# A gated recurrence: the diagonal and the first level as one product of 256 columns, in two halves of the heads

## The chip, the cores and the metric

The kernel runs on one core of a Trainium2 chip. The metric is the device time of one execution in microseconds (us), lower is better.

## What is computed

The reference is four blocks of a small language model over 256 tokens of width 1024, one after another: stick-breaking attention with a convolutional feed-forward block, forgetting attention with another feed-forward block, windowed attention, and last a gated recurrence. Only this last block is touched by the change. Cut to what matters:

```
q = silu(h @ Wq);  log_f = log(lb + (1-lb)*sigmoid(h @ Wf));  k = 1 - exp(log_f);  v = h @ Wi
S_t = exp(log_f_t) * S_(t-1) + k_t v_t^T          # per head, 8 heads, keys 128, values 128
o_t = q_t . S_t
o   = o * rsqrt(mean(o*o) + eps) * gnorm * silu(h @ Wz)
out = o @ W_out                                   # then rmsnorm and residual
```

Without the state it is a product over pairs: o_t is the sum over s <= t of (q_t . (k_s times the product of the forget factors from s+1 to t)) v_s. That is how the kernel computes it.

## The kernel before, in words

**Weights.** All weight matrices come as one stream of units of 128x2048 numbers. SyncE loads a unit, ScalarE rounds it to its high part (line 491), VectorE subtracts to get the low part (line 970, in `split_lo`, called in order by `split_to`), and TensorE multiplies three times (lines 1739 to 1741). Three units have room at a time, so a high part can be made only when the unit three before it is used up. Each engine works through a list of instructions in the order in which it is written, and semaphores tie the lists together.

**The recurrence in levels.** The 256 tokens of the 8 heads make 16 tiles of 128 tokens ("key tiles": `kk_tiles[i]`, with the query tiles beside them). Inside a tile the pairs (s, t) fall into the diagonal (s = t) and seven levels of block size m = 1, 2, 4, ..., 64: in level n a late block of m tokens looks at the early block beside it. For each level TensorE multiplies all 16 key tiles with the late half of the query tiles (`level`, line 2451, 64 columns each). VectorE then copies the entries that belong to this level into the score tiles (`pick`, line 1632, a copy under a mask) and multiplies queries and keys by the forget factors of their neighbouring block (`decay`, lines 1599 and 1600), with which the next level works. The factors of whole blocks, `totals`, are made by pairwise products (`block_totals`, line 1607, one instruction of 1024 elements and five shorter ones, each waiting for the one before). The diagonal has a product of its own, `level_diagonal` (line 2439): the bare queries `qT` against the same key tiles, 128 columns each, picked by `pick_diagonal` (line 1618). Level 1 uses the queries times their own forget factor, `X[0]`, made by `first_queries` (line 1590). These products are in plain float32, for which the program issues each matmul as two passes (16 matmuls are 32 instructions in the trace).

**Order on TensorE.** The products of the recurrence are put between those of the value and gate projections (`rec_i`, `rec_z`). These are 16 parts of 12 matmuls of 512 columns each (`token_rows`). The table `AFTER` says what follows which part: the diagonal after part 1, level 1 after part 2, level n after part n + 1, the product across the two tiles of a head (`cross`) after part 9, the outputs (`outputs(0)`, `outputs(1)`, lines 2472 and 2475) after part 10, the transposes of the first half of the gated outputs (`turn_outputs(0)`, line 2486) after part 15. After part 16 comes the output projection, `last_rows`, which waits for `olo`, the low part of the transposed outputs (line 1711).

**Order on VectorE around the change** (by line in the trace): the first queries of heads 0 to 3 (1590), the scaling of the second half of the queries out of PSUM (1124, two instructions), a split (970), the first queries of heads 4 to 7 (1590), a split (970), `pick_diagonal` (1618, two instructions), `block_totals` (1607), `decay(1)`, `pick(1)`, a split, and so on. After the outputs: sums and means of squares (1686, 1689), whose power -1/2 GpSimd takes (469), a split (`split_to(ro)`), the outputs scaled out of PSUM (`out_scaled`, line 1696, four instructions), the scaling of the gate's first half (1109), `gain_gate` (1678), which waits for a Silu on ScalarE, `out_gated` (1705), two splits, `out_lo` (1711).

**PSUM.** `psD` has four banks of 512 columns. Levels alternate between banks 0, 1 and banks 2, 3, and level n waits until the pick of level n - 2 has read its banks (`rec["picked"]`).

Of the kernel before, what the change touches and what calls it, by code (L numbers as in the profile page):

```python
# [27 lines left out]
ACT = mybir.ActivationFunctionType  # L28
AX = mybir.AxisListType

P = 128
D = 1024
T = 256
TT = T // P
# [7 lines left out]
REC_H = 8  # L42
# [46 lines left out]
def build(nc, stream, pvec, post_g, x_in, wf, bf, b_in, b_out, sinks, gnorm, pos, out):  # L89
    with ExitStack() as ctx:  # L90
# [3 lines left out]
        def sem(name):  # L94
            return ctx.enter_context(nc.semaphore(name))
# [10 lines left out]
        qT = sb("qT", [P, KT, T])  # L106
# [4 lines left out]
        arena = sb("arena", [P, 11264])  # L111
# [93 lines left out]
              for s in ("fox", "win")]  # L205
# [1 line left out]
        rope = {n: sem(f"rope_{n}") for n in ("arg", "sin", "applied", "turned", "copied")}  # L207
        gate = {n: sem(f"gate_{n}") for n in ("z", "tanh", "made")}
        ffn = [{n: sem(f"ffn{i}_{n}") for n in ("scaled", "centre", "tap1", "gate", "up", "gelu", "g", "g_hi", "g_lo")} for i in range(2)]
        rec = {n: sem(f"rec_{n}") for n in ("bound", "bounds", "sigmoid", "silu", "cleared", "ready", "decayed", "total", "level", "cross", "crossed",  # L210
                                            "picked", "gate", "o", "osq", "sums", "omean", "oscale", "scaled", "gated", "turned", "ohi", "olo")}
        stored = sem("stored")

# [261 lines left out]
        def _(act):  # L475
# [415 lines left out]
            def query_silu(c):  # L891

                act.wait_ge(chunk_freed_v, V_FREED[E0["rec_q"] + c])
                part = qT[:, 4 * c:4 * c + 4, :]
                nc.scalar.activation(part, part, ACT.Silu).then_inc(rec["silu"], 1)

            def gate_silu(c):

# [51 lines left out]
        def _(dve):  # L950
# [8 lines left out]
            V = nc.vector  # L959
# [157 lines left out]
            def evac_features(name, c, dst, scale=None, signal=None, first=0):  # L1117

                chunk_wait(name, c)
                for b in range(2):  # L1120
                    k = 4 * (c - first) + 2 * b
                    src, out_ = along(bank(E0[name] + c, b)), dst[:, k:k + 2, :]
                    if scale is None:
                        ins = V.tensor_tensor(out_, src, row_bc, ALU.mult)
                    else:
                        ins = V.scalar_tensor_tensor(out_, src, scale, row_bc, ALU.mult, ALU.mult)
                    if signal is not None and b == 0:
                        ins.then_inc(signal, 1)
                ins.then_inc(chunk_freed_v, 1)
                if signal is not None:  # L1130
                    dve.wait_ge(chunk_freed_v, V_FREED[E0[name] + c])
                    V.memset(st[:, 0, 3, :], 0.0).then_inc(signal, 1)
# [446 lines left out]
                    ins = V.tensor_scalar(head(kk, k), head(kk, k), lbv[:, 2, k:k + 1], None, ALU.mult)  # L1579
                ins.then_inc(rec["ready"], 1)  # L1580

            q_all = qT[:, :, :].rearrange("p k t -> p (k t)")
            QA = X[0]

            def first_queries(c):

                half = slice(1024 * c, 1024 * c + 1024)
                dve.wait_ge(rec["silu"], c + 1)
                dve.wait_ge(rec["ready"], c + 1)
                V.tensor_tensor(QA[:, half], q_all[:, half], keep_f[:, half], ALU.mult).then_inc(rec["decayed"], 1)  # L1590
# [12 lines left out]
            def block_totals():  # L1603

                for n in range(1, 7):
                    total = totals[n - 1].rearrange("p (b two) -> p b two", two=2)
                    V.tensor_tensor(totals[n], total[:, :, 0], total[:, :, 1], ALU.mult).then_inc(rec["total"], 1)
                    dve.wait_ge(rec["total"], n)

            tiles = sc_diag.rearrange("p (g t) -> p g t", t=P)  # L1610

            def pick_diagonal():

                dve.wait_ge(consts_pool, N_CONSTS)
                dve.wait_ge(rec["level"], 1)
                dve.wait_ge(rec["cleared"], 1)
                for half in range(2):
                    ins = V.copy_predicated(tiles[:, 8 * half:8 * half + 8, :], mask_level[:, 0, :].unsqueeze(1).to_broadcast([P, 8, P]),
                                            psD_rows[:, half, :].rearrange("p (g t) -> p g t", t=P))
                ins.then_inc(rec["picked"], 1)  # L1620

            def pick(n):

                m = LEVELS[n - 1]
                nb = P // (2 * m)
                dve.wait_ge(rec["level"], n + 1)
                dve.wait_ge(rec["picked"], n)
                out_ = tiles.rearrange("p g (b two m) -> p g b two m", two=2, m=m)[:, :, :, 1, :]
                mask = mask_level[:, n, :].rearrange("p (b two m) -> p b two m", two=2, m=m)[:, :, 1, :]
                at = 2 * (n % 2)  # L1630
                got = psD[:, at:at + 2, :].rearrange("p k n -> p (k n)").rearrange("p (g b m) -> p g b m", b=nb, m=m)
                V.copy_predicated(out_, mask.unsqueeze(1).to_broadcast([P, TT * REC_H, nb, m]), got).then_inc(rec["picked"], 1)
# [10 lines left out]
            evac_features("rec_q", 0, qT)  # L1643
            split_to(ri + 1)
            first_queries(0)
            evac_features("rec_q", 1, qT)
            split_to(ri + 2)
            first_queries(1)
            split_to(ri + 3)
            pick_diagonal()  # L1650
            block_totals()
            decay(1)
            pick(1)
            split_to(ri + 4)
            decay(2)
            pick(2)
# [56 lines left out]

            out_mean(0)
            out_mean(1)
            split_to(ro)
            out_scaled(0)
            out_scaled(1)
            evac("rec_z", 0, hn[:, 0, 0:512], 5)
            gain_gate(0)  # L1720
            out_gated(0)
# [12 lines left out]
        def _(pe):  # L1734
# [696 lines left out]

            kk_tiles, query_tiles = ([a[:, P * i:P * i + P] for i in range(TT * REC_H)] for a in (kk, X[0]))

            def level_diagonal():

                pe.wait_ge(rec["ready"], 2)
                pe.wait_ge(rec["silu"], 2)
                for i in range(TT * REC_H):
                    ins = MM(psD[:, i // 4, P * (i % 4):P * (i % 4) + P], kk_tiles[i], qT[:, i // 2, P * (i % 2):P * (i % 2) + P],
                             start=(i % 4 == 0), stop=True, skip_group_check=True)  # L2440
                ins.then_inc(rec["level"], 1)

            def level(n):

                m = LEVELS[n - 1]
                pe.wait_ge(rec["decayed"], n + 1)
                pe.wait_ge(rec["picked"], max(n - 1, 1))
                for i in range(TT * REC_H):
                    late = query_tiles[i].rearrange("p (b two m) -> p b two m", two=2, m=m)[:, :, 1, :]
                    at = 64 * (i % 8)  # L2450
                    ins = MM(psD[:, 2 * (n % 2) + i // 8, at:at + 64].rearrange("p (b m) -> p b m", m=m), kk_tiles[i], late,  # L2451
                             start=(i % 8 == 0), stop=True, skip_group_check=True)
                ins.then_inc(rec["level"], 1)
# [25 lines left out]
            def turn_outputs(b):  # L2479
# [3 lines left out]
                for tt in range(TT):  # L2483
                    pe.wait_ge(rec["gated"], 2 * b + tt + 1)
                    for k in range(4):
# [1 line left out]
                                                  X[1][:, tt * D + 512 * b + k * P:tt * D + 512 * b + k * P + P], ident[:, :])  # L2487
                    ins.then_inc(rec["turned"], 1)

            AFTER = {1: [level_diagonal], 2: [lambda: level(1)], 3: [lambda: level(2)], 4: [lambda: level(3)], 5: [lambda: level(4)],  # L2490
                     6: [lambda: level(5)], 7: [lambda: level(6)], 8: [lambda: level(7)], 9: [cross],
                     10: [lambda: outputs(0), lambda: outputs(1)], 15: [lambda: turn_outputs(0)]}
            part = 0
            for name, c in (("rec_i", 0), ("rec_i", 1), ("rec_z", 0), ("rec_z", 1)):
                e = E0[name] + c
# [119 lines left out]
```

## Time and profile before

| | |
|---|---|
| time, median of 3 runs | 911.25 us (911.05 to 911.58) |
| the profiled execution's own time | 911.09 us |
| its span in the trace | 909.4 us |
| TensorE (matmul) busy | 892.2 us, 98% |
| TensorE weight loads busy | 807.1 us, 89% |
| VectorE busy | 654.7 us, 72% |
| ScalarE busy | 486.2 us, 53% |
| GpSimd busy | 47.2 us, 5% |

The span is what the trace covers; the execution's own time is 1.7 us longer. Busy shares are means over stages that have different limits. Matmuls overlap each other in the pipeline, so the distance between the starts of two instructions says what one costs, and not its own duration.

### The profile page before, as it was taken

To read this page: it belongs to the slowest core of one execution; us is meant where nothing else is said; L and a number is where in the kernel's file an instruction comes from. 1 tells how busy PE (TensorE), PEld (TensorE's weight loads), DVE (VectorE), ACT (ScalarE), POOL (GpSimd) and SP (SyncE) were. 2 spreads that over 40 slices of the span, in tenths; PEclk is the share of its full clock that TensorE was granted. 3 is DMA by queue.
4 is the path that set the end of the run, shared out by engine and by line. 5 is a ranking of instruction groups with operands and counts; after the bars stand their busy time and mean duration, and the time that the engine had idled before them with its cause. 6 is when DMAs were issued, how large, how long until landed. Compare 5 with 4: busy or idle time off the path is not lost.

```text
span 909.4 us, 15736 instructions
## 1 busy us (share of the span) xinstructions
PE 892.2 (98%) x6260; PEld 807.1 (89%) x6260; DVE 654.7 (72%) x903; ACT 486.2 (53%) x704; POOL 47.2 (5%) x86
## 2 busy tenths in 40 slices
PE   8999999999999999999999999999999999999997
PEld 7999889999999899888899999998778779988986
DVE  5756558877777886666598768778677776798684
ACT  6555647654654673655565455455636567521252
POOL 2900000000000010000100000000100001000000
PEclk9999999999999999999999999999999999999999
DMA  7553325555455355323264554654443234532221
GB/s 278 194 173 139 140 93 177 217 191 205 159 195 204 139 180 186 139 94 139 94 249 151 226 185 144 225 186 169 162 142 136 95 139 162 186 139 93 94 93 47
DMA packets 21801, 144.51 MB, mean 159 GB/s; under 512 B 2816, under 2 KB 2832, under 8 KB 5104
## 3 DMA queue, kind: packets, MB, share of 16 engines
q1 hardware_dynamic: 20160, 139.47, 43.0%
q0 software_dynamic: 1296, 4.19, 1.6%
q8 instruction: 42, 0.69, 0.3%
q14 instruction: 15, 0.12, 0.0%
q10 hardware_dynamic: 288, 0.04, 0.0%
HBM read 142.64 MB, written 1.05 MB: 158 GB/s over the span
## 4 chain that ended last, share of the span: by engine, by line
PE 89%; DVE 5%; ACT 2%; issue 1%; DMA 1%; POOL 0%; DVEq 0%; SPq 0%; POOLq 0%; ACTq 0%
PE psC L1739 20%; PE psC L1740 19%; PE psC L1741 19%; PE psD L1739 4%; PE psD L1740 4%; PE psD L1741 4%; PE psD L2451 2%; PE psC L1837 2%; PE psC L1839 2%; PE psC L1846 2%; DVE w_lo L970 1%; PE psD L2079 1%; PE psD L2056 1%; PE psD L2068 1%; PE psD L2109 1%
## 5 line engine op out<-in xcount | busy, mean ns | idle before, releaser
L970 DVE TENSOR_TENSOR w_lo<-raw,w_hi 128x2048 fp32r<-128x2048 f32 x125 | 285.5, 2287 | 61.0 <-ACT w_hi L491 60.3
L491 ACT ACTIVATE w_hi<-raw 128x2048 fp32r<-128x2048 f32 x125 | 238.6, 1913 | 81.3 <-PE psC L1741 70.0
L1739 PE MATMUL psC<-xT_hi,w_hi 128*128 128x256 f32 x960 | 273.3, 285 | 0.0
L1740 PE MATMUL psC<-xT_lo,w_hi 128*128 128x256 f32 x960 | 271.6, 283 | 0.0
L1741 PE MATMUL psC<-xT_hi,w_lo 128*128 128x256 f32 x960 | 271.5, 283 | 0.0
L1739 PEld LDWEIGHTS psC<-xT_hi,w_hi 128*128 128x128 f32 x960 | 184.0, 192 | 2.5 <-issue 1.9
L1740 PEld LDWEIGHTS psC<-xT_lo,w_hi 128*128 128x128 f32 x960 | 184.1, 192 | 0.6
L1741 PEld LDWEIGHTS psC<-xT_hi,w_lo 128*128 128x128 f32 x960 | 184.1, 192 | 0.0
L610 ACT ACTIVATE arena<-arena,pv 128x256 f32<-128x256 f32 x88 | 45.8, 591 | 95.1 <-DVE arena L1141 95.1
L1151 DVE SCALAR_TENSOR_TENSOR arena<-arena,pv 128x254 f32<-128x254 f32 (+1 forms) x176 | 75.4, 480 | 20.9 <-ACT arena L610 16.6
L1739 PE MATMUL psD<-w_hi,oT_hi 128*128 128x512 f32 x208 | 81.5, 392 | 0.6 <-DVE w_lo L970 0.6
L1740 PE MATMUL psD<-w_lo,oT_hi 128*128 128x512 f32 x208 | 81.2, 390 | 0.0
L1741 PE MATMUL psD<-w_hi,oT_lo 128*128 128x512 f32 x208 | 80.9, 389 | 0.0
L1739 PE MATMUL psC<-w_hi,xT_hi 128*128 128x256 f32 (+1 forms) x224 | 76.7, 342 | 2.4 <-DVE w_lo L970 2.4
L1741 PE MATMUL psC<-w_hi,xT_lo 128*128 128x256 f32 (+1 forms) x224 | 73.7, 329 | 0.0
L1740 PE MATMUL psC<-w_lo,xT_hi 128*128 128x256 f32 (+1 forms) x224 | 73.6, 328 | 0.0
L1739 PEld LDWEIGHTS psC<-w_hi,xT_hi 128*128 128x128 f32 x224 | 42.5, 190 | 8.2 <-issue 4.0
L1739 PEld LDWEIGHTS psD<-w_hi,oT_hi 128*128 128x128 f32 x208 | 39.1, 188 | 9.2 <-DVE w_lo L970 1.4
L1141 DVE TENSOR_TENSOR arena<-psC,scale_row 128x512 f32<-128x512 f32 x44 | 28.3, 686 | 25.3 <-PE psC L1741 25.2
L1741 PEld LDWEIGHTS psD<-w_hi,oT_lo 128*128 128x128 f32 x208 | 39.1, 188 | 8.3
L1741 PEld LDWEIGHTS psC<-w_hi,xT_lo 128*128 128x128 f32 x224 | 42.5, 190 | 4.0
L1740 PEld LDWEIGHTS psD<-w_lo,oT_hi 128*128 128x128 f32 x208 | 39.1, 188 | 7.3
(312 smaller groups left out, 1345.3 us busy)
## 6 DMA issues: line engine op xcount, KB each, us to landing
raw<-stream SPq DMA_DIRECT2D x130, 1024.0 KB, 4.8
gbc<-post_g POOLq DMA_DIRECT2D x6, 512.0 KB, 4.3
h<-x_in SPq DMA_DIRECT2D x2, 512.0 KB, 5.6
raw<-stream SPq DMA_DIRECT2D x4, 256.0 KB, 7.4
out<-h SPq DMA_DIRECT2D x4, 256.0 KB, 2.0
arena<-b_in POOLq DMA_DIRECT2D x1, 640.0 KB, 4.9
pv<-pvec POOLq DMA_DIRECT2D x1, 176.0 KB, 8.9
arena<-wf POOLq DMA_DIRECT2D x2, 64.0 KB, 2.8
```

The costliest lines, as they stand in the source:

```text
L491: nc.scalar.activation(w_hi[:, slot, :], raw[:, raw_slot, :], ACT.Copy).then_inc(hi_done, 1)
L610: ins = nc.scalar.activation(cv[:, par, g, a, :], xs[:, g, a, :], ACT.Identity, scale=pv[:, bass.ds(at + 2, 1)], bias=pv[:, bass.ds(at + 3 ...
L970: V.tensor_tensor(w_lo[:, slot, :], raw[:, raw_slot, :], w_hi[:, slot, :].bitcast(F32), ALU.subtract).then_inc(lo_done, 1)
L1141: V.tensor_tensor(xs[:, g], along(psC[:, 2 * (e % 2) + g, :]), row_bc, ALU.mult).then_inc(f["scaled"], 1)
L1151: ins = V.scalar_tensor_tensor(y, xs[:, g, a, 0:T - back], pv[:, bass.ds(at + 2 - back, 1)], y, ALU.mult, ALU.add)
L1739: MM(out, lhs[0], rhs[0], start=start, stop=False, skip_group_check=True)
L1740: MM(out, lhs[0], rhs[1], start=False, stop=False, skip_group_check=True)
L1741: return MM(out, lhs[1], rhs[0], start=False, stop=stop, skip_group_check=True)
L1837: MM(out(a), hi[:, k, a * P:a * P + P], xt[0][:, kk_, :], start=(kk_ == 0 and a % 2 == 0), stop=False, skip_group_check=True)
L1839: MM(out(a), lo[:, k, a * P:a * P + P], xt[0][:, kk_, :], start=False, stop=False, skip_group_check=True)
L1846: ins = MM(out(a), hi[:, k, a * P:a * P + P], xt[1][:, kk_, :], start=False, stop=(kk_ == KT - 1), skip_group_check=True)
L2451: ins = MM(psD[:, 2 * (n % 2) + i // 8, at:at + 64].rearrange("p (b m) -> p b m", m=m), kk_tiles[i], late, start=(i % 8 == 0), stop=True, ...
```

## The change

The two products after parts 1 and 2 (the diagonal, level 1) become one product, `first_level(half)`, of 256 columns per key tile: 128 columns of bare queries and 128 of queries times their forget factor, read as two stretches of the arena. For this ScalarE's Silu writes the bare queries to `X[1]`, which lies right behind `X[0]`, instead of back into `qT`. The product is made in two halves, key tiles 0 to 7 (heads 0 to 3) after part 1 and tiles 8 to 15 after part 2. Each half fills all four banks of `psD`, so the second waits for the pick of the first. `pick_first(half)` takes the diagonal out of the one 128 columns and then, after a wait for itself, the odd rows of level 1 out of the other 128. All later products move back by one part in `AFTER`: level n from part n + 1 to part n + 2, `cross` from 9 to 10, the outputs from 10 to 11. `turn_outputs(0)` stays after part 15. On VectorE `block_totals` moves from behind the pick of the diagonal to behind the first queries of heads 0 to 3, and `out_scaled` moves ahead of `split_to(ro)`.

```diff
--- before.py
+++ after.py
@@ -207,7 +207,7 @@
         rope = {n: sem(f"rope_{n}") for n in ("arg", "sin", "applied", "turned", "copied")}
         gate = {n: sem(f"gate_{n}") for n in ("z", "tanh", "made")}
         ffn = [{n: sem(f"ffn{i}_{n}") for n in ("scaled", "centre", "tap1", "gate", "up", "gelu", "g", "g_hi", "g_lo")} for i in range(2)]
-        rec = {n: sem(f"rec_{n}") for n in ("bound", "bounds", "sigmoid", "silu", "cleared", "ready", "decayed", "total", "level", "cross", "crossed",
+        rec = {n: sem(f"rec_{n}") for n in ("bound", "bounds", "sigmoid", "silu", "cleared", "ready", "decayed", "total", "level", "same", "cross", "crossed",
                                             "picked", "gate", "o", "osq", "sums", "omean", "oscale", "scaled", "gated", "turned", "ohi", "olo")}
         stored = sem("stored")
 
@@ -891,8 +891,8 @@
             def query_silu(c):
 
                 act.wait_ge(chunk_freed_v, V_FREED[E0["rec_q"] + c])
-                part = qT[:, 4 * c:4 * c + 4, :]
-                nc.scalar.activation(part, part, ACT.Silu).then_inc(rec["silu"], 1)
+                part = qT[:, 4 * c:4 * c + 4, :].rearrange("p k t -> p (k t)")
+                nc.scalar.activation(X[1][:, 1024 * c:1024 * c + 1024], part, ACT.Silu).then_inc(rec["silu"], 1)
 
             def gate_silu(c):
 
@@ -1579,7 +1579,7 @@
                     ins = V.tensor_scalar(head(kk, k), head(kk, k), lbv[:, 2, k:k + 1], None, ALU.mult)
                 ins.then_inc(rec["ready"], 1)
 
-            q_all = qT[:, :, :].rearrange("p k t -> p (k t)")
+            q_all = X[1]
             QA = X[0]
 
             def first_queries(c):
@@ -1609,15 +1609,20 @@
 
             tiles = sc_diag.rearrange("p (g t) -> p g t", t=P)
 
-            def pick_diagonal():
-
-                dve.wait_ge(consts_pool, N_CONSTS)
-                dve.wait_ge(rec["level"], 1)
-                dve.wait_ge(rec["cleared"], 1)
-                for half in range(2):
-                    ins = V.copy_predicated(tiles[:, 8 * half:8 * half + 8, :], mask_level[:, 0, :].unsqueeze(1).to_broadcast([P, 8, P]),
-                                            psD_rows[:, half, :].rearrange("p (g t) -> p g t", t=P))
-                ins.then_inc(rec["picked"], 1)
+            def pick_first(half):
+
+                if half == 0:
+                    dve.wait_ge(consts_pool, N_CONSTS)
+                    dve.wait_ge(rec["cleared"], 1)
+                dve.wait_ge(rec["level"], half + 1)
+                got = psD[:, :, :].rearrange("p k n -> p (k n)").rearrange("p (g two n) -> p g two n", two=2, n=P)
+                out_ = tiles[:, 8 * half:8 * half + 8, :]
+                V.copy_predicated(out_, mask_level[:, 0, :].unsqueeze(1).to_broadcast([P, 8, P]),
+                                  got[:, :, 1, :]).then_inc(rec["same"], 1)
+                dve.wait_ge(rec["same"], half + 1)
+                out_, got = (a.rearrange("p g (b two) -> p g b two", two=2)[:, :, :, 1] for a in (out_, got[:, :, 0, :]))
+                mask = mask_level[:, 1, :].rearrange("p (b two) -> p b two", two=2)[:, :, 1]
+                V.copy_predicated(out_, mask.unsqueeze(1).to_broadcast([P, 8, 64]), got).then_inc(rec["picked"], 1)
 
             def pick(n):
 
@@ -1643,14 +1648,14 @@
             evac_features("rec_q", 0, qT)
             split_to(ri + 1)
             first_queries(0)
+            block_totals()
             evac_features("rec_q", 1, qT)
             split_to(ri + 2)
             first_queries(1)
             split_to(ri + 3)
-            pick_diagonal()
-            block_totals()
+            pick_first(0)
             decay(1)
-            pick(1)
+            pick_first(1)
             split_to(ri + 4)
             decay(2)
             pick(2)
@@ -1713,9 +1718,9 @@
 
             out_mean(0)
             out_mean(1)
-            split_to(ro)
             out_scaled(0)
             out_scaled(1)
+            split_to(ro)
             evac("rec_z", 0, hn[:, 0, 0:512], 5)
             gain_gate(0)
             out_gated(0)
@@ -2431,20 +2436,24 @@
 
             kk_tiles, query_tiles = ([a[:, P * i:P * i + P] for i in range(TT * REC_H)] for a in (kk, X[0]))
 
-            def level_diagonal():
-
-                pe.wait_ge(rec["ready"], 2)
-                pe.wait_ge(rec["silu"], 2)
-                for i in range(TT * REC_H):
-                    ins = MM(psD[:, i // 4, P * (i % 4):P * (i % 4) + P], kk_tiles[i], qT[:, i // 2, P * (i % 2):P * (i % 2) + P],
-                             start=(i % 4 == 0), stop=True, skip_group_check=True)
+            def first_level(half):
+
+                pe.wait_ge(rec["ready"], half + 1)
+                pe.wait_ge(rec["decayed"], half + 1)
+                if half:
+                    pe.wait_ge(rec["picked"], 1)
+                for i in range(8):
+                    t = 8 * half + i
+                    queries_ = arena[:, 4096 + P * t:8192 + P * t].rearrange("p (two n) -> p two n", two=2)[:, :, 0:P]
+                    ins = MM(psD[:, i // 2, 256 * (i % 2):256 * (i % 2) + 256].rearrange("p (two n) -> p two n", two=2), kk_tiles[t],
+                             queries_, start=(i % 2 == 0), stop=True, skip_group_check=True)
                 ins.then_inc(rec["level"], 1)
 
             def level(n):
 
                 m = LEVELS[n - 1]
                 pe.wait_ge(rec["decayed"], n + 1)
-                pe.wait_ge(rec["picked"], max(n - 1, 1))
+                pe.wait_ge(rec["picked"], max(n - 1, 2))
                 for i in range(TT * REC_H):
                     late = query_tiles[i].rearrange("p (b two m) -> p b two m", two=2, m=m)[:, :, 1, :]
                     at = 64 * (i % 8)
@@ -2487,9 +2496,9 @@
                                                   X[1][:, tt * D + 512 * b + k * P:tt * D + 512 * b + k * P + P], ident[:, :])
                     ins.then_inc(rec["turned"], 1)
 
-            AFTER = {1: [level_diagonal], 2: [lambda: level(1)], 3: [lambda: level(2)], 4: [lambda: level(3)], 5: [lambda: level(4)],
-                     6: [lambda: level(5)], 7: [lambda: level(6)], 8: [lambda: level(7)], 9: [cross],
-                     10: [lambda: outputs(0), lambda: outputs(1)], 15: [lambda: turn_outputs(0)]}
+            AFTER = {1: [lambda: first_level(0)], 2: [lambda: first_level(1)], 4: [lambda: level(2)], 5: [lambda: level(3)],
+                     6: [lambda: level(4)], 7: [lambda: level(5)], 8: [lambda: level(6)], 9: [lambda: level(7)], 10: [cross],
+                     11: [lambda: outputs(0), lambda: outputs(1)], 15: [lambda: turn_outputs(0)]}
             part = 0
             for name, c in (("rec_i", 0), ("rec_i", 1), ("rec_z", 0), ("rec_z", 1)):
                 e = E0[name] + c
```

## Rows read from the trace of the kernel before

**Rows 1.** The page: the chain of work that ended last, its share by engine.
```profile
PE 89%; DVE 5%; ACT 2%; issue 1%; DMA 1%; POOL 0%; DVEq 0%; SPq 0%; POOLq 0%; ACTq 0%
```

**Rows 2.** Timeline of TensorE, parts 1 to 4: start, us, instruction, count, [idle before].
```profile
802.18 3.79 PE L2439 MATMUL psD<-qT,arena 128*128 128x128 f32 x32
...
805.73 0.48 PE L1739 MATMUL psC<-w_hi,xT_hi 128*128 128x512 f32 x1
...
808.32 0.39 PE L1741 MATMUL psC<-w_hi,xT_lo 128*128 128x512 f32 x1
809.03 0.63 PE L2451 MATMUL psD<-arena 128*128 128x64 f32 x4 [0.32 <-DVE arena L1618]
...
812.60 0.48 PE L1739 MATMUL psC<-w_hi,xT_hi 128*128 128x512 f32 x1
...
815.45 0.78 PE L2451 MATMUL psD<-arena 128*128 128x64 f32 x6
...
822.06 0.55 PE L2451 MATMUL psD<-arena 128*128 128x64 f32 x3
```

**Rows 3.** Timeline of TensorE, a float32 product of 256 columns.
```profile
21.28 0.59 PE L1779 MATMUL psD<-scale_diag,neg_ones 128*128 128x256 f32 x2
...
21.83 0.28 PE L1921 MATMUL psC<-xT_hi,w_lo 128*128 128x256 f32 x1
```

**Rows 4.** Timeline of VectorE from the first queries to level 4.
```profile
797.48 1.22 DVE L1590 TENSOR_TENSOR arena<-qT,arena 128x1024 f32<-128x1024 f32 x1
799.64 1.29 DVE L1124 TENSOR_TENSOR qT<-psC,scale_row 128x512 f32<-128x512 f32 x2 [0.94 <-PE psC L1741]
800.84 2.28 DVE L970 TENSOR_TENSOR w_lo<-raw,w_hi 128x2048 fp32r<-128x2048 f32 x1
...
804.18 2.28 DVE L970 TENSOR_TENSOR w_lo<-raw,w_hi 128x2048 fp32r<-128x2048 f32 x1
806.38 2.50 DVE L1618 COPY_PREDICATED arena<-mask_level,psD 128x1024 f32<-128x1024 int8 x2
808.78 1.21 DVE L1607 TENSOR_TENSOR kT<-arena 128x1024 f32<-128x1024 f32 x1
810.02 1.97 DVE L1607 TENSOR_TENSOR kT<-kT 128x512 f32<-128x512 f32 x5
812.89 1.23 DVE L1599 TENSOR_TENSOR arena<-arena 128x1024 f32<-128x1024 f32 x1 [0.91 <-PE psD L2451]
...
815.17 2.45 DVE L1632 COPY_PREDICATED arena<-mask_level,psD 128x1024 f32<-128x1024 int8 x1
...
828.16 1.24 DVE L1632 COPY_PREDICATED arena<-mask_level,psD 128x1024 f32<-128x1024 int8 x1
```

**Rows 5.** Timeline of TensorE from the end of the outputs to the output projection.
```profile
863.61 0.48 PE L1739 MATMUL psC<-w_hi,xT_hi 128*128 128x512 f32 x1
...
877.34 1.04 PE L2486 MATMUL psC<-ident,arena 128*128 128x128 f32 x8
...
880.95 0.45 PE L1739 MATMUL psD<-w_hi,oT_hi 128*128 128x512 f32 x1
```

**Rows 6.** Timeline of GpSimd, the second power of the outputs' means.
```profile
866.09 1.64 POOL L469 TENSOR_TENSOR rst<-rst,minus_half 128x8 f32<-128x8 f32 x1 [1.90 <-DVE rst L1689]
```

**Rows 7.** Timeline of VectorE from the scaled outputs to their low part.
```profile
869.02 2.48 DVE L1696 TENSOR_TENSOR arena<-psD,rst 128x512 f32<-128x512 f32 x4
871.42 0.74 DVE L1109 TENSOR_SCALAR hn<-psC,st 128x512 f32<-128x512 f32 x1
...
874.55 1.29 DVE L1705 TENSOR_TENSOR arena<-arena,hn 128x512 f32<-128x512 f32 x2
...
880.17 1.28 DVE L1711 TENSOR_TENSOR oT_lo<-psC,oT_hi 128x512 fp32r<-128x512 f32 x2
```

**Rows 8.** Timeline of TensorE, its longest idle stretch between two instructions.
```profile
8.94 0.66 PE L1759 MATMUL psC<-ident,h 128*128 128x128 f32 x4 [2.13 <-DMA h<-x_in]
```

**Rows 9.** Windows: busy time of each engine, PEclk (1.00 is 2.4 GHz), DMA, GB/s.
```profile
5.00:10.00 5.00, 2.87 (x18) 2.47 (x19) 0.00 (x0) 2.53 (x7) 0.00 (x0) 1.00 0.97 343
```

## Prediction, made before the result was known

> **What bounds the kernel now.** I read the chain of waits on the page first: TensorE holds 89% of it, VectorE 5%, ScalarE 2% [rows 1]. So time is won or lost only where TensorE works less or stands still. Then the timelines of the recurrence, engine by engine. The reader is to see two places where TensorE and VectorE already meet with nothing to spare. First, level 1: part 2's last matmul starts at 808.32 and the level at 809.03, after a wait for `pick_diagonal` (L1618) [rows 2]; VectorE works through from 799.64 to 811.99, without a pause [rows 4]. Second, the end of the block: VectorE's low part of the transposed outputs starts at 880.17 and its first instruction takes 1.28 / 2 = 0.64, so it is there at 880.8; the output projection that waits for it starts at 880.95 [rows 5, 7]. The change moves VectorE's work at the first place and TensorE's at the second.
>
> **TensorE's own work.** A float32 pass of 256 columns: L1779 has two passes in 0.59 us and the next group but one starts 21.83 - 21.28 = 0.55 later, with one f32r matmul of 256 columns (about 0.12) in between [rows 3]. So a pass costs (0.55 - 0.12) / 2 = 0.215. Before, 32 passes of 128 columns take 805.73 - 802.18 = 3.55, that is 0.11 each, and level 1 with 64 columns 812.60 - 809.03 = 3.57, the same [rows 2]: there the weight load sets the pace. The change puts 32 passes of 0.215 = 6.9 in place of 3.55 + 3.57 = 7.1. Saved: 0.2. Bounds for a pass: 0.11 (the pace of the narrow ones), 0.3 (half of the 0.59). I take 0.215, the row of the same type and width. A half costs 3.45.
>
> **VectorE up to the first pick.** Costs are distances between starts [rows 4]. The first queries of heads 0 to 3 start at 797.48. A first-queries instruction with a split costs 804.18 - 800.84 = 3.34, a split alone 806.38 - 804.18 = 2.20, so the former 1.14. From 798.62 on, in the new order: `block_totals`, 811.99 - 808.78 = 3.21, to 801.83. The 0.94 pause before 799.64 hides part of it. Scaling of the queries 1.20, to 803.03. Split and first queries 3.34, to 806.37 (ScalarE's Silu has from 803.1 to 805.2 for its work, and it now writes to `X[1]` at the same size: nothing). Split 2.20, to 808.57. Then `pick_first(0)`: the diagonal's copy of 1024 elements is half of 2.50, 1.25, with the wait for itself 1.30. The second copy takes 512 elements, every second one. The trace has no such form. The pick of level 1 takes 2.45 for 1024 elements in single-element steps, that of level 3 takes 1.24 for as many in runs of four. Bounds: 0.62 (half of 1.24) and 2.45 (each element at twice the slow pace, should the stride in PSUM cost as well). I take half of 2.45, 1.23, since its mask and target step by two as before. `pick_first(0)` ends at 808.57 + 1.30 + 1.23 = 811.10.
>
> Here a rule of the Trainium skill speaks for the change (SBUF — State Buffer, "Door 1: The DMA port swizzle"): accesses that hit a 16-byte line at least twice keep full bandwidth, so a stride of two in float32 would be free. By it the copy would take 0.62 and the sum below would be lower by 0.6. The pick of level 1, with two hits a line, takes twice as long as that of level 3 [rows 4]: the trace does not bear the rule out for this instruction.
>
> **The first stall.** TensorE: product half 0 from 802.18 to 805.65, part 2 of 815.45 - 812.60 = 2.85 [rows 2], done at 808.5. Half 1 overwrites the banks of half 0 and so waits for the pick. Release takes 809.03 - 808.88 = 0.15 (the pick of the diagonal ran from 806.38 for 2.50) [rows 2, 4], so half 1 starts at 811.25: 2.75 of standing still, where 0.48 stood before (809.03 less the end of part 2 at 808.32 + 0.23). Behind that wait stand parts 3 and up. Half 1 ends at 814.7. Parts 3 and 4 take 2.85 + 2.73, to 820.3. In that time VectorE does `decay(1)` from 815.0 (it starts 0.29 after the level's end, as 812.89 after 812.60) for 815.17 - 812.89 = 2.28, and `pick_first(1)` for 2.53, to 819.8: 0.3 ahead of level 2, so nothing more is lost. Before, level 2 starts at 815.45 with one part less done (2.73). The shift is 820.3 - 815.45 - 2.73 = 2.1. One loss goes: level 3 starts at 822.06, though 815.45 + 3.49 (a level) + 2.85 is 821.79; now two parts instead of one give VectorE room before level 2, and its split stands ahead of `decay(2)` while TensorE is still in level 2. That gives back 0.27. **First term: +1.9.** From there all levels and parts have the old rhythm, since each level still has one part behind it.
>
> **The second stall.** The outputs now end after part 11. The end, at 863.61 before [rows 5], comes at 863.61 + 2.73 + 1.9 = 868.2. From there TensorE has four parts before the transposes in place of five, VectorE the same chain. Before: from the outputs' end to the scaling of the gate (871.42) 7.81 [rows 5, 7]. After: the means are done 2.4 after the end (GpSimd starts 866.09 - 863.61 = 2.48 after it [rows 6]); `out_scaled(0)`, half of 871.42 - 869.02 = 2.40, to 3.6; `out_scaled(1)` waits for the power, which ends at 2.48 + 1.64 = 4.1, to 5.4; the split of 2.20, to 7.6. The new order gains 0.2 alone, because ScalarE and GpSimd set the pace in either one. The gate's scaling starts at 868.2 + 7.6 = 875.8, 4.4 later than before. What comes then on VectorE (Silu's wait, gain, `out_gated`, two splits, `out_lo`) is as it was: 880.8 + 4.4 = 885.2, and the projection starts at 880.95 + 4.4 = 885.4. TensorE gets there early: four parts (4 x 2.73 + 0.1 = 11.0) to 879.2, a wait of 0.5 for `out_gated` (874.55 + 0.64 + 4.4 = 879.6), transposes of 0.8 and part 16 (2.8) to 883.3. It then stands for 2.0. **Second term: +2.5**, 4.4 less the 1.9 already counted. After it nothing changes: the second gated half has the same distance to its transposes.
>
> **Sum.** 0.2 of saved matmuls is inside the first term. The profiled execution's 911.09 + 4.4 = 915.5; the median of the runs is 0.16 above it: 915.6.
>
> **Rivals.**
> *A, only the first stall.* If VectorE's chain behind the outputs were not what the projection waits for: 911.25 + 1.9 = 913.1. For it: `out_scaled` stands sooner. Against: 880.8 against 880.95 [rows 5, 7], the chain has no slack for a part that moved ahead of the outputs.
> *B, a wide pass at the pace of a narrow one, 0.11.* Each half is then 1.7 shorter. Half 0's gain is lost in the stall, half 1's stays: 915.6 - 1.7 = 913.9. Against: 0.215 [rows 3].
> *C, the clock falls while TensorE stands.* Half 1 at 1.2 GHz takes 6.9 in place of 3.45: 915.6 + 3.45 = 919.0. For it: the stall of 2.75 is longer than any idle stretch of the trace. Against: after 2.13 of idle at 6.8 to 8.94 the clock is still 1.00 [rows 8, 9].
> *D, the change does what it says, faster.* The bank wait is hidden, because `pick_first(0)` is half as wide as the old pick and the totals leave the way between pick and decay. Then 0.48 and 0.27 of waiting and 0.2 of matmul go: 910.3. It decides at one point: the pick must be through at 808.4, 2.7 before my 811.1; and behind the outputs VectorE must not be the later one. For it: VectorE pauses for 0.91 before `decay(1)` and 0.94 before the scaling [rows 4]. Against: only the second pause lies ahead of the pick, and 3.21 moves ahead of it.
> *E, no change* would need 4.4 of errors in two places to cancel.
>
> **How the numbers follow.** My forecast with its sizes 0.70, A 0.10, B 0.04, C 0.06, D 0.08, E 0.02. The second copy's bounds move the sum by -0.6 and +1.2 (both terms stand on the first pick's end): 915.0 to 916.8. I widen to 912.9, which takes in A and B, and to 917.2, leaving out C, D and E: 0.16. A difference of 0.2% (1.8 us) is about what a measurement of this kernel tells from none; A at +1.9 lies at its edge, and I count most of it as slower. Faster 0.07, same 0.04, slower 0.89.
>
> **What would show it.** In the changed trace: two stretches of idle on TensorE, about 2.7 ahead of the second wide product with VectorE's masked copy as its releaser, and about 2 ahead of the output projection with `out_lo` as its releaser, with a short one of 0.5 before the transposes. Wide passes at a distance of 0.215. Both second copies at about 1.2. VectorE's scaling of the gate some 7.6 after the outputs' end. Wrong would be: no idle ahead of the second product (D), passes at 0.11 (B), a PEclk below 1.00 after 811 (C), or a projection that starts right behind part 16 (A).

## The result, and the profile after

The changed kernel takes 917.1 us (median of five executions, 915.2 to 919.1; a sixth took 3056.9 us and is left out) against 911.5 us before (median of six, 911.05 to 912.0). The ratio is 1.006, with a 95% interval of 1.0049 to 1.0072: slower, by 4.5 to 6.6 us. The profiled execution took 915.9 us, span 914.1. The forecast was 915.6 us, within 912.9 to 917.2.

The page of the changed kernel: TensorE has the same busy time as before in 32 fewer instructions, and VectorE's chain has a larger share of what ended last (9% where it was 5% [rows 1]):

```profile
PE 892.6 (98%) x6228; PEld 806.9 (88%) x6228; DVE 655.1 (72%) x904; ACT 485.9 (53%) x704; POOL 47.5 (5%) x86
...
PE 83%; DVE 9%; ACT 3%; issue 2%; DMA 1%; POOL 1%; DVEq 0%; SPq 0%; POOLq 0%; ACTq 0%
```

TensorE's timeline of the changed kernel, where [rows 2, 5] stood before. Its first line is the start of part 1 (799.44 in the kernel before). L2448 is the wide product, L2460 a level, L2495 the transposes, L1744 with `psD` the output projection:

```profile
799.78 0.40 PE L1744 MATMUL psC<-w_hi,xT_hi 128*128 128x512 f32 x1
...
802.53 3.62 PE L2448 MATMUL psD<-arena 128*128 128x256 f32 x16
...
811.71 3.69 PE L2448 MATMUL psD<-arena 128*128 128x256 f32 x16 [2.81 <-DVE arena L1625]
...
820.71 0.56 PE L2460 MATMUL psD<-arena 128*128 128x64 f32 x4
...
827.04 0.67 PE L2460 MATMUL psD<-arena 128*128 128x64 f32 x5
...
880.03 1.17 PE L2495 MATMUL psC<-ident,arena 128*128 128x128 f32 x8 [0.36 <-DVE arena L1710]
...
885.54 0.50 PE L1744 MATMUL psD<-w_hi,oT_hi 128*128 128x512 f32 x1 [1.58 <-DVE oT_lo L1716]
```

The bracket is the idle time in front and who ended it. The three waits are the ones of the prediction: 2.81 before the second half of the wide product, 0.36 before the transposes, 1.58 before the output projection. VectorE's timeline says why the first is there ([rows 4] before):

```profile
797.82 1.22 DVE L1590 TENSOR_TENSOR arena<-arena 128x1024 f32<-128x1024 f32 x1
798.95 1.22 DVE L1607 TENSOR_TENSOR kT<-arena 128x1024 f32<-128x1024 f32 x1
800.21 1.96 DVE L1607 TENSOR_TENSOR kT<-kT 128x512 f32<-128x512 f32 x5
802.20 1.29 DVE L1124 TENSOR_TENSOR qT<-psC,scale_row 128x512 f32<-128x512 f32 x2
803.41 2.28 DVE L970 TENSOR_TENSOR w_lo<-raw,w_hi 128x2048 fp32r<-128x2048 f32 x1
805.61 1.22 DVE L1590 TENSOR_TENSOR arena<-arena 128x1024 f32<-128x1024 f32 x1
806.74 2.28 DVE L970 TENSOR_TENSOR w_lo<-raw,w_hi 128x2048 fp32r<-128x2048 f32 x1
808.94 1.29 DVE L1620 COPY_PREDICATED arena<-mask_level,psD 128x1024 f32<-128x1024 int8 x1
810.27 1.29 DVE L1625 COPY_PREDICATED arena<-mask_level,psD 128x512 f32<-128x512 int8 x1
815.44 1.23 DVE L1599 TENSOR_TENSOR arena<-arena 128x1024 f32<-128x1024 f32 x1 [3.88 <-PE psD L2448]
```

From 797.82 to 811.56 there is no pause that the timeline marks: the totals (L1607) stand in front of everything that the pick needs, and right behind the pick VectorE stands idle for 3.88. And the end of the block, VectorE ([rows 7] before):

```profile
870.81 1.28 DVE L1701 TENSOR_TENSOR arena<-psD,rst 128x512 f32<-128x512 f32 x2
872.65 1.29 DVE L1701 TENSOR_TENSOR arena<-psD,rst 128x512 f32<-128x512 f32 x2 [0.56 <-POOL rst L469]
873.86 2.28 DVE L970 TENSOR_TENSOR w_lo<-raw,w_hi 128x2048 fp32r<-128x2048 f32 x1
876.05 0.74 DVE L1109 TENSOR_SCALAR hn<-psC,st 128x512 f32<-128x512 f32 x1
...
884.80 1.28 DVE L1716 TENSOR_TENSOR oT_lo<-psC,oT_hi 128x512 fp32r<-128x512 f32 x2
```

**A measure that is finer than the time.** Profiles differ by up to 2 us before part 1, where no kernel here has an edit (part 1 starts between 798.81 and 800.80). The difference is there by the first float32 product of 256 columns [rows 3], which starts at 20.57 to 22.61 us; from it to part 1 all thirteen profiles take 778.12 to 778.26. I therefore compare the *block*, from the start of part 1 to the span's end, one profile each. Before: 909.4 - 799.44 = 109.96. Changed: 914.1 - 799.78 = 114.32, which is +4.36. The spans are known to 0.1 us, and no kernel's block was taken often enough to give it an interval, so a tenth or two of it proves nothing.

| kernel | time, median (range) | over before, medians | part 1 starts | span | block over before |
|---|---|---|---|---|---|
| changed, second set (`after_again`) | 917.96 (915.06 to 918.82) | +6.9 | 800.80 | 916.7 | +5.94 |
| warm | 915.21 (914.77 to 916.30) | +4.2 | 799.17 | 913.5 | +4.37 |
| totals_back | 913.54 (912.75 to 914.99) | +2.5 | 799.68 | 911.7 | +2.06 |
| both | 911.96 (911.68 to 913.70) | +0.9 | 799.26 | 910.2 | +0.98 |
| shift_only | 913.85 (912.80 to 915.27) | +2.4 | 798.81 | 911.1 | +2.33 |
| totals_only | 913.51 (912.93 to 915.62) | +2.1 | 799.79 | 911.8 | +2.05 |
| lo_sooner | 914.50 (913.86 to 915.77) | +3.1 | 799.42 | 912.6 | +3.22 |
| scaled_back | 917.62 (915.74 to 919.48) | +6.2 | 799.21 | 915.3 | +6.13 |
| gate_sooner | 912.34 (911.80 to 913.33) | +1.1 | 800.06 | 910.5 | +0.48 |
| spread | 911.89 (911.38 to 912.92) | +0.6 | 799.57 | 909.7 | +0.17 |
| spread2 | 910.82 (910.09 to 912.47) | -0.5 | 798.97 | 908.2 | -0.73 |

The kernel before ran beside them: 911.05 us for the first four rows, 911.44 for the next four, 911.25 for gate_sooner and spread, 911.34 for spread2.

### The profile page after: what moved, and what is told of

It reads as the page before. It is cut to its first block, busy times and chain, and to the rows that moved or that the text cites. A ratio compares the mean times of both kernels' runs of the same rounds, so it can differ in the third digit from the quotient of the medians.

```text
span 914.1 us, 15672 instructions
## 1 busy us (share of the span) xinstructions
PE 892.6 (98%) x6228; PEld 806.9 (88%) x6228; DVE 655.1 (72%) x904; ACT 485.9 (53%) x704; POOL 47.5 (5%) x86
## 4 chain that ended last, share of the span: by engine, by line
PE 83%; DVE 9%; ACT 3%; issue 2%; DMA 1%; POOL 1%; DVEq 0%; SPq 0%; POOLq 0%; ACTq 0%
PE psC L1744 18%; PE psC L1746 17%; PE psC L1745 17%; PE psD L1744 4%; PE psD L1745 4%; PE psD L1746 4%; DVE w_lo L970 3%; PE psD L2460 2%; PE psC L1842 2%; PE psC L1844 2%; PE psC L1851 2%; PE psD L2084 1%; PE psD L2061 1%; ACT w_hi L491 1%; PE psD L2073 1%
## 5 line engine op out<-in xcount | busy, mean ns | idle before, releaser
L1744 PE MATMUL psC<-xT_hi,w_hi 128*128 128x256 f32 x960 | 273.3, 285 | 0.0
L1744 PEld LDWEIGHTS psC<-xT_hi,w_hi 128*128 128x128 f32 x960 | 184.1, 192 | 2.5 <-issue 1.9
L1744 PE MATMUL psD<-w_hi,oT_hi 128*128 128x512 f32 x208 | 81.6, 392 | 2.2 <-DVE oT_lo L1716 1.6
L1744 PE MATMUL psC<-w_hi,xT_hi 128*128 128x256 f32 (+1 forms) x224 | 76.9, 343 | 2.4 <-DVE w_lo L970 2.4
L1744 PEld LDWEIGHTS psC<-w_hi,xT_hi 128*128 128x128 f32 x224 | 42.5, 190 | 8.2 <-issue 3.8
L1744 PEld LDWEIGHTS psD<-w_hi,oT_hi 128*128 128x128 f32 x208 | 39.1, 188 | 11.0 <-DVE oT_lo L1716 2.0
```

What stands on the lines that cost most here:

```text
L1744: MM(out, lhs[0], rhs[0], start=start, stop=False, skip_group_check=True)
```

## The experiments

**1. The part moved ahead of the outputs, alone.** The kernel before, with level 2 to 7, `cross` and the outputs one part later:

```diff
-AFTER = {1: [level_diagonal], 2: [lambda: level(1)], 3: [lambda: level(2)], 4: [lambda: level(3)], 5: [lambda: level(4)],
-         6: [lambda: level(5)], 7: [lambda: level(6)], 8: [lambda: level(7)], 9: [cross],
-         10: [lambda: outputs(0), lambda: outputs(1)], 15: [lambda: turn_outputs(0)]}
+AFTER = {1: [level_diagonal], 2: [lambda: level(1)], 4: [lambda: level(2)], 5: [lambda: level(3)], 6: [lambda: level(4)],
+         7: [lambda: level(5)], 8: [lambda: level(6)], 9: [lambda: level(7)], 10: [cross],
+         11: [lambda: outputs(0), lambda: outputs(1)], 15: [lambda: turn_outputs(0)]}
```

> The kernel before with one edit: levels 2 to 7, the cross product and the outputs one part later, as the change has them; two narrow products, old order on VectorE. My theory (the part moved ahead of the outputs is lost to VectorE's chain behind them): +2.4 us, with a wait of about 2 for out_lo before the output projection. Rival (the later place costs nothing, VectorE has slack): -0.3, the wait before level 3 gone.

Measured: +2.4 us, ratio 1.0027 (1.0017 to 1.0036). Timeline of TensorE of this kernel:

```profile
877.07 1.17 PE L2486 MATMUL psC<-ident,arena 128*128 128x128 f32 x8 [0.62 <-DVE arena L1705]
882.58 0.50 PE L1739 MATMUL psD<-w_hi,oT_hi 128*128 128x512 f32 x1 [1.58 <-DVE oT_lo L1711]
```

No product is wider and no total moved, and yet both late waits are there (0.62 + 1.58 = 2.2). The later place of the levels, `cross` and the outputs makes the second term by itself. The rival is out.

**2. The totals moved, alone.** The kernel before:

```diff
             first_queries(0)
+            block_totals()
...
             pick_diagonal()
-            block_totals()
```

> The kernel before with one edit: block_totals moved to behind the first queries of heads 0 to 3, old products and places. My theory: pick of the diagonal 2.2 later, level 1 waits 2.7 instead of 0.5, the block ends 2.2 later: +2.2 us. Rival (totals off the way between pick and decay(1) give it back at level 2): within 0.3 of before.

Measured: +2.1 us, ratio 1.0024 (1.0015 to 1.0033). The size is right, the place is not:

```profile
804.72 3.81 PE L2439 MATMUL psD<-qT,arena 128*128 128x128 f32 x32 [2.02 <-ACT qT L895]
811.59 3.76 PE L2451 MATMUL psD<-arena 128*128 128x64 f32 x32 [0.31 <-DVE arena L1618]
```

TensorE stands before the diagonal, not before level 1: the totals delay the scaling of the second half of the queries, so ScalarE's Silu of it, and the diagonal needs all queries. I had overlooked that. In the changed kernel the first half does not need them, and the same delay shows one step later, before the second half. In either form it is VectorE that is 2.2 us late: its last split before the pick starts at 806.74 in both, 6.95 and 6.96 after part 1, where it was 4.74 before (804.18 [rows 4]).

**3. The changed kernel with each cause taken away.** Totals behind the pick:

```diff
             first_queries(0)
-            block_totals()
...
             pick_first(0)
+            block_totals()
             decay(1)
```

> The changed kernel with block_totals moved behind pick_first(0), into the time in which VectorE waits for the second half. My theory (the first stall comes from 3.2 us of totals ahead of the pick, 0.9 of it hidden): the stall shrinks from 2.8 to 0.6 and the time is 2.2 below the changed kernel's, +2.3 over before. Rival (the pick itself, or the Silu on ScalarE, is late anyway): under 0.5 gained.

Measured: +2.5 us, 4.4 below the changed kernel's median of the same set; block 2.3 below the first profile of it. The wait is down to what was forecast:

```profile
809.41 3.69 PE L2448 MATMUL psD<-arena 128*128 128x256 f32 x16 [0.62 <-DVE arena L1625]
```

The block gives the 2.2 of my theory; the medians give twice as much. I put that surplus down to the clock: experiment 4, which leaves the wait and keeps the clock up, gains about as much (2.7).

The low part of the outputs between the splits (and the same on ScalarE):

```diff
             out_gated(0)
-            split_to(ro + 2)
+            split_to(ro + 1)
             out_lo(0)
+            split_to(ro + 2)
```

> The changed kernel with out_lo(0) between the two splits, block_totals left where the change has it. My theory: only the 1.6 wait before the output projection goes, the time is 1.6 below the changed kernel's, +3.0 over before. Rival (two stalls share one cause, so removing the second alone gives nothing): no gain.

Measured: +3.1 us; block +3.22, that is 1.14 less than +4.36. So the second stall can be removed without the first; the rival is out. Why it is 1.1 and not 1.6 the next kernel shows, which has both edits:

> block_totals behind pick_first(0), and out_lo(0) with its ScalarE part put between the two splits instead of behind both (a split is 2.2 us). My theory: the first stall down to 0.6, the one before the output projection (1.6) gone: 3.8 below the changed kernel, +0.7 over before (0.4 of it the wait before the transposes). Rival (the chain behind the outputs binds again a step later, at the second transposes): +2.3, no more than totals moved back alone.

Measured: +0.9 us, ratio 1.001 (1.0001 to 1.0019). Its waits on TensorE:

```profile
877.25 1.17 PE L2497 MATMUL psC<-ident,arena 128*128 128x128 f32 x8 [0.36 <-DVE arena L1711]
...
887.19 1.17 PE L2497 MATMUL psC<-ident,arena 128*128 128x128 f32 x8 [0.57 <-DVE arena L1711]
```

The wait before the projection is gone, and a third of it comes back before the second transposes, as the rival said in kind, though not in size: there VectorE's chain binds again, for 0.57. The trace of lo_sooner has the same two waits, 0.9 together. The two edits take 3.4 of the block's 4.4 away.

The old order of `out_scaled`:

```diff
+            split_to(ro)
             out_scaled(0)
             out_scaled(1)
-            split_to(ro)
```

> The changed kernel with split_to(ro) ahead of out_scaled again, as before. My theory: the chain from the outputs' end to the gate's scaling is 0.2 longer (7.8 instead of 7.6), the time 0.2 above the changed kernel's, hardly to be told. Rival (the new order is worth the whole split): 2.2 above it.

Measured: 917.6 us, +6.2 over before; the changed kernel has +5.6 and +6.9 in its two sets, so no difference can be told. Its wait before the transposes is 0.6 in place of 0.4, the 0.2 of the theory, and its block is +6.13 against the +5.94 of `after_again`; both profiles have the low clock of experiment 4. The rival's 2.2 is out.

**4. What the medians have above the profile.** The changed kernel as it is, once more, and one with dummy matmuls where it stands still (the first added line waits until the PSUM columns they write to are free):

```diff
                 if half:
+                    pe.wait_ge(chunk_freed_v, V_FREED[E0["rec_q"] + 1])
+                    stay_warm(psC[:, 2 * ((E0["rec_q"] + 1) % 2), 0:P], 22, neg_tri_r)
```

> The changed kernel as it is, for the spread of its executions: the profile shows 4.7 us more than before, but the runs lie 3.6 to 7.5 above it. Theory S (the two stalls alone): all executions near +4.5 us with a granted clock as before. Theory C (TensorE's stall of 2.8 us lets the clock fall in some executions): the slow ones have the lower mean clock, about 1 us longer for each 0.001 of mean clock.

> The changed kernel with 22 dummy matmuls of 128 columns (about 2.4 us, results unused) on TensorE where it stands still before the second half of the wide product. Theory S: same time as the changed kernel's profiled run, +4.5 us over before, and no narrower spread. Theory C: the spread of several us goes, every execution is near +4.5 and the clock is back at before's.

Measured: 917.96 (six executions, range 3.8) and 915.21 us (five, range 1.5), the latter with a ratio of 1.0045 (1.0032 to 1.0058) to before. With added work the kernel is 2.7 us *faster*. The second profile of the changed kernel shows what can happen in the wait. Windows and TensorE's timeline of it; the last three numbers of a window are PEclk (1.00 is 2.4 GHz, 0.50 is 1.2 GHz), DMA share, GB/s:

```profile
808.00:812.00 4.00, 1.92 (x9) 1.25 (x7) 3.97 (x3) 1.91 (x1) 0.00 (x0) 1.00 0.89 293
812.00:814.00 2.00, 1.29 (x4) 1.11 (x5) 0.57 (x1) 0.00 (x0) 0.00 (x0) 0.75 0.92 389
814.00:816.00 2.00, 2.00 (x7) 1.55 (x6) 0.00 (x0) 0.00 (x0) 0.00 (x0) 0.50 0.17 66
816.00:818.00 2.00, 2.00 (x10) 1.73 (x9) 0.00 (x0) 0.00 (x0) 0.00 (x0) 0.90 0.00 0
```

```profile
812.71 5.38 PE L2448 MATMUL psD<-arena 128*128 128x256 f32 x16 [2.80 <-DVE arena L1625]
```

The first profile of the changed kernel, same wait of 2.81, and the warm one, in the same stretch:

```profile
812.00:814.00 2.00, 2.00 (x11) 1.76 (x10) 0.00 (x0) 0.00 (x0) 0.00 (x0) 1.00 0.67 279
814.00:816.00 2.00, 2.00 (x11) 1.72 (x10) 0.56 (x1) 0.00 (x0) 0.00 (x0) 1.00 0.00 0
```

```profile
808.12 2.57 PE L1752 MATMUL psC<-neg_tri_r 128*128 128x128 f32 x22
811.12 3.69 PE L2451 MATMUL psD<-arena 128*128 128x256 f32 x16 [0.43 <-DVE arena L1625]
```

The same product takes 5.38 in one execution and 3.69 in another. Of the four profiles with a wait of 2.8, two have it at half clock for a stretch (this one and scaled_back's, also 5.38) and two have not (the first, and lo_sooner's with 3.69). The price in the block is 5.94 - 4.36 = 1.6. With TensorE kept busy the block is +4.37, as in the undisturbed profile, and the five executions lie closer together. Theory C holds. Its mean clock is weaker evidence than I had expected. The changed kernel's second set has 0.999 in the fastest execution and 0.994 in the two slowest, but 0.997 at 918.45, and the kernel before has anything from 0.995 to 1.000 within 2.6 us.

The mean clock is blurred by a second place, which I had overlooked. Near the start TensorE waits for the input, and what the clock does there differs from profile to profile. The four transposes before and behind that wait, in the kernel before (behind it: [rows 8]) and in totals_only, whose program is the same there:

```profile
5.75 1.06 PE L1759 MATMUL psD<-ident,h 128*128 128x128 f32 x4
```

```profile
5.73 0.60 PE L1759 MATMUL psD<-ident,h 128*128 128x128 f32 x4
8.46 0.66 PE L1759 MATMUL psC<-ident,h 128*128 128x128 f32 x4 [2.13 <-DMA h<-x_in]
8.96 1.01 PE L1759 MATMUL psD<-ident,h 128*128 128x128 f32 x4
```

Four transposes take 0.60 to 0.66 at the high pace and 1.06 to 1.12 at the low one. In totals_only the pace falls right behind a wait of 2.13, and PEclk is 0.50 from 9.0 to 12.0. Five more profiles show the same fall, in or behind waits of 2.44 to 2.53; one of them is the first profile of the changed kernel, whose mean of 0.998 comes from there and not from its wait of 2.8. In the kernel before the wait is 2.13 too, and the pace rises across it, from 1.06 to 0.66 and then 0.60. Waits of 1.47 to 1.79 in five other profiles show no fall. In `after_again` (1.83) the pace is low up to 14.1 us, although PEclk reads 1.00 there; it is also the profile in which part 1 starts last. How the executions without a trace, up to 3 us above their fastest, divide between the wait of 2.8 and this start stays open.

**5. The order that follows from it.** Three more orders on top of "both". First the gate's scaling ahead of the split:

```diff
             out_scaled(1)
-            split_to(ro)
             evac("rec_z", 0, hn[:, 0, 0:512], 5)
+            split_to(ro)
```

> The kernel with both repairs, and the scaling of the gate's first half ahead of split_to(ro) instead of behind it, so that ScalarE's Silu runs while VectorE splits. My theory (the last waits behind the outputs, 0.4 and 0.6 before the two transposes, come from VectorE's chain): the first of them goes and the time is 0.4 below that kernel, +0.5 over before. Rival (the split is then too late for part 15): no gain or up to 1 slower.

Measured: +1.1 us, ratio 1.0015 (1.0006 to 1.0024), which the median alone would call no gain; the block is 0.5 shorter (+0.48 after +0.98), and the wait before the first transposes is gone. Then VectorE's order in front (`block_totals` now takes its first and last step; that part of the edit is left out here):

```diff
-            split_to(ri + 3)
             pick_first(0)
-            block_totals()
+            split_to(ri + 3)
+            block_totals(1, 1)
             decay(1)
             pick_first(1)
+            block_totals(2, 6)
```

> As the last, and in front VectorE's order is set by what each step waits for: pick_first(0) ahead of the split of a unit that part 5 needs, the first of block_totals' steps into the wait for the second half, the other five behind pick_first(1). My theory: no wait before the second half of the wide product or before level 3, 0.6 less than the last kernel; with 0.2 of saved matmuls and 0.75 of removed waits 0.5 below before. Rival (what is moved behind pick_first(1) makes decay(2) late): +0.5 over before or more, with a wait before level 3.

Measured: +0.6 us, ratio 1.0006 (0.9997 to 1.0015), not 0.5 below. Two waits are left:

```profile
808.87 3.69 PE L2451 MATMUL psD<-arena 128*128 128x256 f32 x16 [0.19 <-DVE arena L1626]
...
886.63 1.17 PE L2498 MATMUL psC<-ident,arena 128*128 128x128 f32 x8 [0.50 <-DVE arena L1712]
```

The last edit treats the second of these as gate_sooner treated the wait before the first transposes:

```diff
             out_lo(0)
-            split_to(ro + 2)
             evac("rec_z", 1, hn[:, 0, 512:1024], 5)
+            split_to(ro + 2)
```

> As the last kernel, and the scaling of the gate's second half ahead of the split of the projection's second unit as well. My theory: the wait of 0.5 before the second transposes goes and the time is 0.3 to 0.5 below the last kernel's, level with before or 0.3 under it. Rival (the split is then late for the projection's second unit): no gain.

Measured: 910.82 against 911.34 us, ratio 0.9997 (0.9988 to 1.0006). The wait is gone and the block is 0.73 shorter than before's, but by the runs this is no difference from before. How much of the 0.73 the wide product itself earns is not shown: the new orders on VectorE could shorten the kernel with two narrow products as well, and that kernel was not run.

## Why the prediction was right

It was right in direction and in mechanism, and its steps are in the trace of the profiled execution almost to the tenth. Where the median came to lie in the range is partly luck (below).

- *Price of a wide pass*, 0.215: the 16 passes of the first half fill 3.62, which is 16 x 0.215 = 3.44 and the part of the last one that overlaps what follows. Measured up to the second matmul of the next part, less its 0.23, the two halves cost 3.46 and 3.53 and the narrow products before 3.64 and 3.65: 0.3 saved, 0.2 forecast. The busy time on the page does not show it (892.6 against 892.2).
- *VectorE up to the first pick*: forecast end 811.10, found 811.56 with part 1 0.34 later. The second copy, of which there was no row, takes 1.29 for 512 elements against the 1.23 that I took. By the rule of the Trainium skill (SBUF — State Buffer, "Door 1: The DMA port swizzle"), a stride of two in float32 is free, and my estimate by it was 0.62: the trace does not agree, here as in the pick of level 1.
- *First term, +1.9*: the wide product's wait 2.81 (forecast 2.75). Level 3 begins at 827.04, 27.26 after part 1 begins; before it was 22.62. Less the extra part of 2.73 this is 1.91.
- *Second term, +2.5*: the gate's scaling comes 4.29 later after part 1 than before (876.05 - 799.78 against 871.42 - 799.44), the projection 4.25 later; the forecast for both was 4.4. Less the first term's 1.91 the second is 2.3. The wait before the projection is 1.58 and not 2.0, since the transposes and part 16 ended 0.3 later than I had reckoned.
- *Sum*: +4.4 forecast, +4.36 in the block of the profiled execution. Rivals A, B and D are out: the last wait is there, a pass costs 0.215 and not 0.11, and the wait ahead of the second half is there. E is out by the interval.

**What was mis-sized is the chance of rival C.** The median of 917.1 lies 1.5 us above the forecast, just inside the range's end of 917.2; the same kernel's second set has 917.96, which lies outside. In a part of the executions the clock does fall behind the wait of 2.8. I had given this 0.06, on the strength of an idle stretch of 2.13 after which the clock was "still" at 1.00 [rows 8, 9]. That was misread: four transposes take 1.06 before the stretch and 0.66 behind it, so there the clock had just risen, and PEclk's 1.00 for 5 to 10 us hides it. In totals_only the pace falls behind a stretch of the same 2.13. Rival C's price was too high in turn: I let the whole half run at 1.2 GHz (3.45), and 1.7 was measured (5.38 against 3.69), since in `after_again` the clock is back at 816.4, before the half is over at 818.1.

## What to carry to other kernels

When a step is moved forward on an engine, go through that engine's list to the next thing that another engine waits for: here 3.2 us of totals were moved forward, 0.9 of them went into a pause and 2.2 became a stall on TensorE. When a product is moved past a part on TensorE, ask whose chain hangs on its result, and whether that chain had the part's length to spare (here 17.2 us of VectorE, ScalarE and GpSimd, 863.61 to 880.8, against 17.3 us of TensorE, 863.61 to 880.95 [rows 5, 7]). A wait of 2.8 us on TensorE cost 1.6 more than itself in some executions here; look at the spread of the runs and not only at one profile, and try dummy work in a wait that must stay.

## What the runs showed of the hardware that was not expected

- The clock fell from 2.4 to 1.2 GHz behind idle stretches of 2.8 us on TensorE in two of four profiles (at 813.0 in `after_again`, whose product begins at 812.71); in both it was back before the product behind the stretch was over, and the cost was 1.7 us on that product. Near the start of the kernel it fell in six of the thirteen profiles, in or behind stretches of 2.13 to 2.53 us. The waits of 2.0 in the block (totals_only) and of 1.6 us (shift_only) show no fall, in one profile each.
- PEclk can read 1.00 in the first microseconds of a profile while the matmuls run at the low pace (`after_again`, 1.12 us for four transposes at 8.55, as in the changed kernel's first profile at PEclk 0.50).
- A masked copy with a stride of two takes as long for 512 elements (1.29) as one without for 1024 (1.29). That the new one reads PSUM with a stride too adds little: the pick of level 1, which reads PSUM without one, takes 2.45 for 1024 [rows 4], half of which is 1.23.
